# Experts of two mixture-of-experts blocks in quads: 32 tokens each, a one-hot gather for each quad, and the next quad's gather behind the down projection

## The chip, the cores and the metric

The kernel runs on one core of a Trainium2 chip. Its engines are TensorE (PE, with its weight loads shown as PEld), VectorE (DVE), ScalarE (ACT), GpSimd (POOL) and SyncE (SP), which issues the transfers here. The metric is the device time of one execution in microseconds (us); lower is better.

## The reference

Two transformer stacks one after the other, two layers each, on 256 tokens of width 1024, all in float32. Every layer has a mixer (attention; or retention, RWKV and a short convolution) and then a mixture of 32 experts. What is computed there, for the first stack:

```python
group_p = softmax(xt @ w_group); group_w, group_id = top_k(group_p, 1)
in_group = take_along_axis(expert_logits, group_id)
top_logits, local_id = top_k(in_group, 2)
gates = group_w * softmax(top_logits)
# for each token t and each of its two experts e:
y[t] += gate * ((silu(x[t] @ w_gate[e]) * (x[t] @ w_up[e])) @ w_down[e])
```

In the first stack there are 8 groups of 4 experts, 256 wide inside; in the second 4 groups of 8, 512 wide. So 512 assignments fall on 32 experts, and an expert can get any number of them from 0 to 256. All experts' weights are read in every layer: 100.7 MB in a layer of the first stack, 201.3 MB in one of the second.

## The kernel before

**Weights** come through `ring`, six slots of 2048 KB (a chunk, 4096 floats in each of 128 partitions). SP issues a chunk when `w_used` says that the chunk six before it has been used; PE waits on the slot's `w_loaded`. An expert of the first stack has one chunk of gate and up weights and half a chunk of down weights; one of the second stack has a chunk each for gate, up and down. Six expert chunks are loaded before the expert stage begins.

**`route`** (L1445) finds the two experts of each token, gives each assignment a slot from 1 to 512, sorted by expert, and gathers all 512 rows at once with PE: `xtok` (tokens by features) times `once` (a one-hot of tokens by slots, made by DVE), 16 matmuls of 512 columns (L1501), copied by ACT to `Xs`. DVE builds `by_slot` (gates by slots) and the tables `offs` and `left`.

**`experts`** (L1583) works on pairs of experts in a window of up to 64 tokens each (`WIN`). DVE copies the pair's two windows out of `Xs` to `Xw` (`windows`, L1712). PE multiplies `Xw` by the weights: each expert has 64 columns of the array and 64 rows of the PSUM bank (L1657). One pair of the first stack is 16 such matmuls (gate and up together, 512 wide), one of the second is 16 for gate and 16 for up. Then PE adds the *previous* pair's result into banks 0 to 3 (`combine`, L1639: `Yw` times `gwT`, the gates by tokens), with the turn of `hid` (L1667) and of `gw` (L1672) between, and does the down projection (L1684), second half of the width first. ACT does the silu (L1704), DVE the product (L1727), and both copy results out (L1708, L1740). A float32 matmul stands in the trace as two records, so 16 matmuls are 32 records.

The loop runs `iters` times (8 turns of two pairs in the first stack, 16 turns of one pair in the second), and again for as many rounds as the largest expert needs windows of 64. The order of work on an engine is the order of the code; engines meet only at semaphores. In a pair the two chunks of a matmul group are released together at its end, and the chunks of the next groups are already in the ring.

**The ada products** (L756), which the change does not touch, are named since the prediction reads them: they use 32 columns of the array each, four in turn, 512 wide, one chunk for 8 matmuls.

## Time and profile before

| | us |
|---|---|
| median of 3 runs | 3320.39 |
| lowest, highest | 3319.87, 3323.3 |
| span of the profiled execution | 3318.3 |
| PE busy | 2797.8 (84%) |
| DVE busy | 855.7 (26%) |
| ACT busy | 472.3 (14%) |
| gate and up matmuls (L1657), 3072 records | 703.6 |
| down matmuls (L1684), 1536 records | 343.7 |
| sums into banks 0 to 3 (L1639), 1088 records | 263.5 |
| HBM read | 777.00 MB, 234 GB/s over the span |

The profile is of one execution, by the hardware profiler. Busy time is a union: matmuls that run side by side count once. In a timeline row stand the start, the busy time, the engine, the line, the operation with its output and inputs, and the count of records merged in the row; in brackets the engine's idle time before it and what ended it. The granted clock of TensorE is given as a share of 2.4 GHz; it has two levels, 1.2 and 2.4 GHz, so 0.90 over a stretch means that a fifth of it ran at the lower one.

### The profile page before, as it was taken

The page shows a single profiled execution, that of the slowest core. Times are in us where ns is not written, and L with a number is a line of the kernel's source. Part 1 is how long each engine was busy: PE and PEld are TensorE (multiplying, and loading weights), DVE is VectorE, ACT ScalarE, POOL GpSimd, SP SyncE. Part 2 cuts the span into 40 slices and gives each one's busy share as a digit, 9 for nine tenths or more (in the row PEclk, how much of TensorE's full clock was granted, in tenths as well). Part 3 has the DMA queues.
Part 4 walks back from the last instruction along what each step waited for, and adds up shares of the span by engine and source line. Part 5 has one row for each costly group of instructions (what it writes and reads, how often), then busy time and mean ns, then how long its engine had stood idle before and what let it go on. Part 6 is the DMA issues. An engine that isn't in the chain of part 4 may idle for free. (4 is left out here: it accounts for less than half of the span.)

```text
span 3318.3 us, 34187 instructions
## 1 busy us (share of the span) xinstructions
PE 2797.8 (84%) x13108; PEld 1699.9 (51%) x13108; DVE 855.7 (26%) x1849; ACT 472.3 (14%) x879; POOL 0.2 (0%) x4
## 2 busy tenths in 40 slices
PE   6869997868996994869898889869858797988886
PEld 4544445544443852858743333347547686333333
DVE  1442221343122126351121111111364312110111
ACT  1311110321111002200111011010121001101111
POOL 0000000000000000000000000000000000000000
PEclk9889998888998997969989999989978798999998
DMA  6015995114994553003349999864700032899994
GB/s 266 32 54 215 428 419 217 51 46 166 427 428 189 236 192 163 1 1 129 150 191 429 428 429 428 374 276 166 289 1 1 26 152 105 368 429 429 428 429 206
DMA packets 55690, 779.39 MB, mean 235 GB/s; under 512 B 6825, under 2 KB 7081, under 8 KB 7849
## 3 DMA queue, kind: packets, MB, share of 16 engines
q1 hardware_dynamic: 55592, 778.07, 56.4%
q8 instruction: 64, 1.05, 0.1%
q14 instruction: 34, 0.27, 0.0%
HBM read 777.00 MB, written 1.05 MB: 234 GB/s over the span
## 5 line engine op out<-in xcount | busy, mean ns | idle before, releaser
L1657 PE MATMUL bank<-ring,arena 128*64 128x512 f32 x3072 | 703.6, 612 | 84.6 <-issue 70.1
L1657 PEld LDWEIGHTS bank<-ring,arena 128*64 128x64 f32 x3072 | 240.8, 141 | 538.7 <-issue 538.4
L1684 PE MATMUL bank<-ring,arena 128*64 128x512 f32 x1536 | 343.7, 596 | 0.0
L1639 PE MATMUL bank<-arena 128*128 128x256 f32 x1088 | 263.5, 386 | 3.6 <-DVE arena L1740 3.6
L1639 PEld LDWEIGHTS bank<-arena 128*128 128x128 f32 x1088 | 196.1, 190 | 80.2 <-issue 58.9
L1727 DVE TENSOR_TENSOR arena<-bank,arena 128x256 f32<-128x256 f32 (+1 forms) x64 | 35.7, 558 | 776.6 <-ACT arena L1704 776.6
L825 PE MATMUL bank<-xnT,ring 128*128 128x256 f32 x960 | 211.4, 383 | 9.3 <-PEq L271 9.3
L1684 PEld LDWEIGHTS bank<-ring,arena 128*64 128x64 f32 x1536 | 104.6, 137 | 193.5 <-issue 193.5
L825 PEld LDWEIGHTS bank<-xnT,ring 128*128 128x128 f32 x960 | 184.6, 193 | 35.9 <-issue 10.3
L1357 PE MATMUL bank<-xnT,ring 128*128 128x256 f32 x768 | 177.1, 384 | 23.8 <-PEq L962 23.8
L1357 PEld LDWEIGHTS bank<-xnT,ring 128*128 128x128 f32 x768 | 148.1, 193 | 46.1 <-issue 25.4
L1704 ACT ACTIVATE arena<-bank 128x256 f32<-128x256 f32 (+1 forms) x64 | 31.4, 491 | 843.7 <-PE bank L1657 843.7
L295 PE MATMUL bank<-arena,cst 128*128 128x256 f32 x160 | 51.2, 490 | 85.9 <-ACT arena L280 85.9
L1740 DVE COPY arena<-bank 128x512 f32<-128x512 f32 x64 | 44.3, 692 | 305.1 <-PE bank L1684 305.1
L1364 PE MATMUL bank<-arena,ring 128*128 128x256 f32 x384 | 90.7, 379 | 0.0
L295 PEld LDWEIGHTS bank<-arena,cst 128*128 128x128 f32 x160 | 39.6, 254 | 98.9 <-ACT arena L280 91.3
L674 PE MATMUL bank<-arena,ring 128*128 128x256 f32 x256 | 59.7, 398 | 33.5 <-DVE arena L688 33.5
L819 PE MATMUL bank<-ring,xnT 128*128 128x512 f32 x192 | 82.7, 592 | 0.0
L1501 PE MATMUL bank<-arena 128*128 128x512 f32 x128 | 63.7, 661 | 19.7 <-DVE arena L1554 19.7
L831 DVE COPY arena<-bank 128x512 f32<-128x512 f32 x20 | 13.8, 692 | 249.2 <-PE bank L825 176.8
L1364 PEld LDWEIGHTS bank<-arena,ring 128*128 128x128 f32 x384 | 73.0, 190 | 9.9
L1708 ACT COPY arena<-bank 128x512 f32<-128x512 f32 x64 | 37.5, 586 | 269.0 <-PE bank L1684 269.0
(335 smaller groups left out, 2822.9 us busy)
## 6 DMA issues: line engine op xcount, KB each, us to landing
ring<-in_w_exp SPq DMA_DIRECT2D x288, 2048.0 KB, 15.5
ring<-in_w_ada SPq DMA_DIRECT2D x24, 2048.0 KB, 7.9
ring<-in_w_in SPq DMA_DIRECT2D x20, 2048.0 KB, 11.3
ring<-in_w_merge SPq DMA_DIRECT2D x18, 2048.0 KB, 17.1
ring<-in_w_o SPq DMA_DIRECT2D x8, 2048.0 KB, 16.4
ring<-in_w_conv SPq DMA_DIRECT2D x6, 2048.0 KB, 27.5
ring<-in_w_rest SPq DMA_DIRECT2D x2, 1696.0 KB, 21.1
small<-in_small SPq DMA_DIRECT2D x2, 1440.0 KB, 22.9
```

The source lines that it names most:

```text
L295: last = nc.tensor.matmul(sums[:, 0:T], K("ones"), sq[:, k, :], start=k == 0, stop=k == KT - 1)
L674: last = nc.tensor.matmul(bank[b][:, T * (j % 2):T * (j % 2) + T], w[:, k, P * j:P * j + P], mixT[:, k, :], start=k == 0, stop=k == KT - 1)
L819: last = nc.tensor.matmul(o[:, 0:MW], xnT[:, k, P * (not first):P * (not first) + P], w[:, k, :], start=k == 0, stop=k == KT - 1)
L825: last = nc.tensor.matmul(o[:, T * j:T * j + T], w[:, k, col:col + P], xnT[:, k, :], start=k == 0, stop=k == KT - 1)
L1357: last = nc.tensor.matmul(bank[m % 8][:, 0:T], w[:, k, P * (d % 4):P * (d % 4) + P], xnT[:, k, :], start=k == 0, stop=k == KT - 1)
L1364: last = nc.tensor.matmul(bank[m % 8][:, T:2 * T], w[:, k, P * d:P * d + P], ys[i][:, k, :], start=k == 0, stop=k == MT - 1)
L1501: last = nc.tensor.matmul(bank[gather_banks[d]][:, :], xtok[:, t, P * d:P * d + P], once[:, t, :], start=t == 0, stop=t == TT - 1)
L1639: nc.tensor.matmul(bank[d // 2][:, T * (d % 2):T * (d % 2) + T], Yw[:, P * d:P * d + P], gwT, start=False, stop=False, skip_group_check=True)
L1657: last = nc.tensor.matmul(o[rows(e), 0:MW], Xw[:, k, WIN * e:WIN * e + WIN], ring[:, slot(n), MW * k:MW * k + MW], start=k == 0, stop=k == ...
L1684: last = nc.tensor.matmul(o[rows(e), :], hidT[:, j, WIN * e:WIN * e + WIN], ring[:, slot(n), at:at + MW], start=j == 0, stop=j == ft - 1)
L1708: nc.scalar.copy(Yw[:, MW:D], y1_bank[:, :]).then_inc(y1_taken, 1)
L1740: nc.vector.tensor_copy(Yw[:, 0:MW], y0_bank[:, :]).then_inc(y0_taken, 1)
```

## The change

`route` and `experts` become one function, `moe` (L1447 of the new file). Experts run four at a time ("quad"), each in a window of 32 tokens: 32 columns of the array and 32 rows of the bank. What one pass over a quad does is an *item*. A quad whose largest expert has more than 32 tokens gets a second item (and so on), with its weights kept in the ring; the number of items and each item's quad are worked out by DVE from the counts, and read from `offs` and `meta` by the other engines.

There is no gather of all tokens. Each item has a one-hot of its own (`onehot`, tokens by 128 slots, made by DVE from a table of ranks), and PE gathers with 16 matmuls of 128 columns (L1535), into banks 6 and 7; the gather of the next item stands behind the down projection. ACT and DVE copy the halves to `Xw`. Gate, up and down of all four experts run with the experts inside the loop over k, so in the second stack an item is a group of 32 matmuls on four chunks for gate, the same for up, the same for down. The weights in memory are laid out in quads; the ring keeps its six slots. The sum of the previous item now stands in one piece ahead of the turn of `hid`. The zeroing of banks 0 to 3 moves ahead of the ranks, the last matmul that only closed the sum is gone, and the last additions to `hT` start bank by bank.

```diff
-        WIN = 64
+        WIN = 32
+        QUAD = 4
+        NQ = NE // QUAD
         ROUNDS = T // WIN
-        SLOTS = 2 * T
...
+        ITEMS = NQ + 2 * T // WIN
+        xtok = ar(0, TT, D)
+        Xw = ar(2048, KT, P)
...
+                    sp.wait_ge(tables_ready, 1)
+                    for q in range(NQ):
+                        if q:
+                            earlier = sp.value_load(offs[0:1, LAST_AT + q - 1:LAST_AT + q], min_val=0, max_val=ITEMS * per_turn)
+                        if per_turn > RING:
+                            same = sp.value_load(offs[0:1, LAST_AT + q:LAST_AT + q + 1], min_val=0, max_val=ITEMS * per_turn)
+                        for n in range(RING if q == 0 else 0, per_turn):
+                            if n < RING:
+                                sp.wait_ge(w_used, earlier + (n0 + n + per_turn - RING + 1))
+                            else:
+                                sp.wait_ge(w_used, same + (n0 + n - RING + 1))
+                            sp.dma_start(ring[:, slot(n), :], feed(q, n)).then_inc(w_loaded[slot(n)], 16)
...
+                    def gather():
+                        for d in range(KT):
+                            for t in range(TT):
+                                last = nc.tensor.matmul(gather_banks[d // 4][:, P * (d % 4):P * (d % 4) + P], xtok[:, t, P * d:P * d + P], onehot[:, t, :],
+                                                        start=t == 0, stop=t == TT - 1)
+                            if d == 3:
+                                last.then_inc(low_gathered, 1)
+                        last.then_inc(high_gathered, 1)
...
+                        pe.wait_ge(low_taken, it + 1)
+                        pe.wait_ge(high_taken, it + 1)
+                        pe.wait_ge(y1_taken, it + 1)
+                        for o, first in ((gate_bank, 0),) if shared else ((gate_bank, 0), (up_bank, QUAD)):
+                            if first:
+                                pe.wait_ge(y0_taken, it + 1)
+                            for e in range(QUAD):
+                                here(first + e)
+                            for k in range(KT):
+                                for e in range(QUAD):
+                                    last = nc.tensor.matmul(o[rows(e), :], Xw[:, k, rows(e)], ring[:, slot(first + e), MW * k:MW * k + MW],
+                                                            start=k == 0, stop=k == KT - 1)
+                                    if k == KT - 1:
+                                        last.then_inc(w_used, 1)
+                        pe.wait_ge(y0_taken, it + 1)
+                        pe.wait_ge(gwT_ready, it + 1)
+                        combine()
+                        pe.wait_ge(hid_made, it + 1)
+                        for j in range(ft):
+                            last = nc.tensor.transpose(gate_bank[:, P * j:P * j + P], hid[:, P * j:P * j + P], K("ident"))
+                        last.then_inc(hid_turned, 1)
+                        pe.wait_ge(gw_ready, it + 1)
...
+                        pe.wait_ge(hidT_ready, it + 1)
+                        for n in range(n_gu, per_turn):
+                            here(n)
+                        for half, o in ((1, y1_bank), (0, y0_bank)):
+                            if half == 0:
+                                pe.wait_ge(gwT_ready, it + 2)
+                            for j in range(ft):
+                                for e in range(QUAD):
+                                    n, at = (n_gu + e // 2, ft * D * (e % 2)) if shared else (n_gu + e, 0)
+                                    at += D * j + MW * half
+                                    last = nc.tensor.matmul(o[rows(e), :], hidT[:, j, rows(e)], ring[:, slot(n), at:at + MW], start=j == 0, stop=j == ft - 1)
+                                    if half == 0 and j == ft - 1 and (e % 2 == 1 or not shared):
+                                        last.then_inc(w_used, 1)
+                            if half == 1:
+                                last.then_inc(y1_done, 1)
+                        if more:
+                            pe.wait_ge(onehot_ready, it + 2)
+                            gather()
...
+                    then(nc.vector.tensor_reduce(most, count.rearrange("p (q e) -> p q e", e=QUAD), AX, ALU.max))
+                    then(nc.vector.tensor_scalar(most, most, 1.0 / WIN, None, ALU.mult))
+                    then(nc.vector.tensor_tensor(more, most.unsqueeze(2).broadcast_to([P, NQ, ROUNDS - 1]), iota[:, 0:ROUNDS - 1].unsqueeze(1).broadcast_to([P, NQ, ROUNDS - 1]), ALU.is_gt))
+                    then(nc.vector.tensor_reduce(rounds, more, AX, ALU.add))
+                    then(nc.vector.tensor_scalar(rounds, rounds, 1.0, None, ALU.add))
...
-                                for k in range(KT):
-                                    for e, n in enumerate((wa, wb)):
-                                        last = nc.tensor.matmul(o[rows(e), 0:MW], Xw[:, k, WIN * e:WIN * e + WIN], ring[:, slot(n), MW * k:MW * k + MW],
-                                                                start=k == 0, stop=k == KT - 1)
-                                        if k == KT - 1:
-                                            last.then_inc(w_used, 1)
...
+                        if more:
+                            dve.wait_ge(low_gathered, it + 1)
+                            dve.wait_ge(high_gathered, it + 1)
+                            dve.wait_ge(gw_ready, it + 1)
+                            off = dve.value_load(offs[0:1, bass.ds(RANK_AT + it + 1, 1)], min_val=0, max_val=NE * TT * ROUNDS - QUAD * TT)
+                            slots_of(rank_tab[:, bass.ds(off, QUAD * TT)])
```

Of PE's instructions in the second stack's expert loop, before (L1657 gate, then up; L1639 the sum; L1667 and L1672 turns; L1684 down, its two halves):

```order
L1657 MATMUL bank<-ring,arena 64x512 x16
L1645 REGISTER_ALU
L1657 MATMUL bank<-ring,arena 64x512 x16
L1639 MATMUL bank<-arena 128x256 x4
L1667 MATMUL bank<-cst,arena 128x128 x4
L1639 MATMUL bank<-arena 128x256 x4
L1672 MATMUL bank<-cst,arena 128x128 x2
L1684 MATMUL bank<-ring,arena 64x512 x8
L1680 REGISTER_ALU
L1684 MATMUL bank<-ring,arena 64x512 x8
```

and in the changed kernel (L1567 gate and up, L1543 the sum, L1576 and L1580 turns, L1592 down, L1535 the next gather):

```order
L1567 MATMUL bank<-ring,arena 32x512 x64
L1543 MATMUL bank<-arena 128x256 x8
L1576 MATMUL bank<-cst,arena 128x128 x4
L1580 MATMUL bank<-cst,arena 128x128 x2
L1555 REGISTER_ALU
L1592 MATMUL bank<-ring,arena 32x512 x16
L1587 REGISTER_ALU
L1592 MATMUL bank<-ring,arena 32x512 x16
L1535 MATMUL bank<-arena 128x128 x16
```

The count of matmuls per expert is the same (8 for gate, 8 for up, 8 for down); a loop turn now holds four experts for two, the sum comes once a turn in one piece, and the gather has moved into the loop.

The same engine between the router's logits and the first expert, before:

```order
L1484 MATMUL bank<-cst,xnT 128x128 x16
L1490 MATMUL bank<-arena,cst 128x32
L1491 MATMUL bank<-arena,cst 128x32
L1492 MATMUL bank<-arena,cst 128x32
L1494 MATMUL bank<-arena,cst 128x32 x2
L1501 MATMUL bank<-arena 128x512 x16
L1468 UNCONDITIONAL_BRANCH
L1634 UNCONDITIONAL_BRANCH
L1642 MATMUL bank<-cst 128x512 x4
L1607 TENSOR_LOAD meta
```

and in the changed kernel:

```order
L1516 MATMUL bank<-cst,xnT 128x128 x16
L1519 MATMUL bank<-cst 128x512 x4
L1525 MATMUL bank<-arena,cst 128x32
L1526 MATMUL bank<-arena,cst 128x32
L1527 MATMUL bank<-arena,cst 128x32
L1529 MATMUL bank<-arena,cst 128x32 x2
L1535 MATMUL bank<-arena 128x128 x16
L1480 TENSOR_LOAD meta
```

The zero matmuls (L1642, now L1519) stand ahead of the ranks, the gather is a quarter as wide, and no block ends between it and the experts.

## Rows read from the trace of the kernel before

**Rows 1.** The page: its first line, and the rate in 40 slices.
```profile
span 3318.3 us, 34187 instructions
GB/s 266 32 54 215 428 419 217 51 46 166 427 428 189 236 192 163 1 1 129 150 191 429 428 429 428 374 276 166 289 1 1 26 152 105 368 429 429 428 429 206
```

**Rows 2.** Windows: length, busy time of five engines, PEclk, DMA share, GB/s.
```profile
400.00:420.00 20.00, 20.00 (x94) 9.35 (x91) 3.73 (x9) 1.73 (x4) 0.00 (x0) 1.00 1.01 429
...
500.00:520.00 20.00, 17.79 (x80) 9.39 (x76) 4.30 (x11) 1.34 (x3) 0.00 (x0) 1.00 0.00 0
...
1800.00:1900.00 100.00, 91.29 (x412) 37.50 (x410) 10.51 (x22) 11.03 (x14) 0.00 (x0) 0.97 1.01 428
```

**Rows 3.** Timeline: start and end of an expert stage of each stack, SP's first issue.
```profile
280.37 7.09 PE L1657 MATMUL bank<-ring,arena 128*64 128x512 f32 x32
...
287.78 7.92 SPq L1624 DMA_DIRECT2D ring<-in_w_exp  x3
...
518.71 2.73 DVE L1745 TENSOR_TENSOR hT<-hT,bank 128x256 f32<-128x256 f32 x8 [4.73 <-PE bank L1694]
...
1696.88 13.96 PE L1657 MATMUL bank<-ring,arena 128*64 128x512 f32 x64
...
2163.52 3.23 DVE L1747 SCALAR_TENSOR_TENSOR hT<-bank,mod,hT 128x256 f32<-128x256 f32 x8 [4.73 <-PE bank L1694]
```

**Rows 4.** Two chunk issues of L187 by themselves: start, and time to landing.
```profile
L187 SPq DMA_DIRECT2D ring<-in_w_ada x1: 333/333/333, 2297.8 to 2297.8; - x1
DMA to landing us min/median/max: 7.8/7.8/7.8
...
L187 SPq DMA_DIRECT2D ring<-in_w_ada x1: 333/333/333, 2304.7 to 2304.7; - x1
DMA to landing us min/median/max: 7.7/7.7/7.7
```

**Rows 5.** Timeline of PE in the ada products, 32-column matmuls, lower and full clock.
```profile
1069.93 3.35 PE L756 MATMUL bank<-ring,arena 128*32 128x512 f32 x16 [3.03 <-DMA ring<-in_w_ada]
...
1074.82 1.93 PE L756 MATMUL bank<-ring,arena 128*32 128x512 f32 x16 [0.56 <-DMA ring<-in_w_ada]
```

**Rows 6.** Timeline of PE in the second stack, two phases after waits.
```profile
2960.98 7.09 PE L1657 MATMUL bank<-ring,arena 128*64 128x512 f32 x32 [1.22 <-DMA ring<-in_w_exp]
2970.73 8.74 PE L1657 MATMUL bank<-ring,arena 128*64 128x512 f32 x32 [2.66 <-issue]
```

**Rows 7.** Windows that start with dense matmuls after a wait.
```profile
33.00:53.00 20.00, 19.96 (x80) 17.16 (x81) 0.69 (x1) 0.59 (x1) 0.00 (x0) 0.86 1.01 428
...
259.80:279.80 20.00, 19.01 (x39) 8.21 (x40) 8.89 (x36) 5.55 (x10) 0.00 (x0) 0.90 0.01 2
```

**Rows 8.** Windows soon after the expert transfers start, first stack's second layer.
```profile
825.00:830.00 5.00, 5.00 (x26) 3.75 (x26) 2.27 (x6) 0.76 (x2) 0.00 (x0) 1.00 0.99 383
830.00:835.00 5.00, 5.00 (x26) 1.59 (x23) 0.73 (x2) 0.59 (x1) 0.00 (x0) 1.00 1.00 413
```

**Rows 9.** Timeline at the end of the first layer's experts.
```profile
505.50 1.99 PE L1639 MATMUL bank<-arena 128*128 128x256 f32 x8
...
509.59 3.65 PE L1684 MATMUL bank<-ring,arena 128*64 128x512 f32 x16
...
514.13 3.69 PE L1639 MATMUL bank<-arena 128*128 128x256 f32 x16 [0.89 <-DVE arena L1740]
```

**Rows 10.** Timeline of the first layer's routing.
```profile
250.39 3.53 PE L1484 MATMUL bank<-cst,xnT 128*128 128x128 f32 x16
...
255.07 0.19 DVE L1542 COPY arena<-bank 128x32 f32<-128x32 f32 x1 [1.99 <-PE bank L1494]
...
257.27 0.48 DVE L1553 TENSOR_SCALAR arena<-arena 128x512 f32<-128x512 f32 x1
...
259.88 15.97 PE L1501 MATMUL bank<-arena 128*128 128x512 f32 x32 [4.92 <-DVE arena L1554]
...
276.76 3.67 PE L1642 MATMUL bank<-cst 128*128 128x512 f32 x8 [0.92 <-PEq L1468]
```

More of the change, by code:

```diff
@@ L1458, in route, with slot, items, used @@
             gs, ge, pen = (ar(at + 100 + 16 * i, TT, ng) for i in range(3))
[L1459 to L1467 removed]
+            gtop, gsum, coef = (ar(at + 160 + 2 * i, TT, 1) for i in range(3))
+            z, zs, ez, sel = (ar(at + 200 + 64 * i, TT, NE) for i in range(4))
+            v8 = ar(at + 520, TT, 8)
+            d21 = ar(at + 540, TT, 1)
+            count = ar(at + 560, NE)
+            most, rounds, cum = (ar(at + 600 + 8 * i, NQ) for i in range(3))
+            more = ar(at + 640, NQ, ROUNDS - 1)
+            past = ar(at + 720, ITEMS + 1, NQ)
+            quad_of, before_it = (ar(at + 930 + 32 * i, ITEMS + 1) for i in range(2))
+            gate_bank, up_bank = bank[4], bank[4 if shared else 5]
+            y1_bank, y0_bank = bank[4], bank[5]
+            gather_banks = (bank[6], bank[7])
+            iota = K("iota")
+            def slot(n):
+                return (n0 + n) % RING
+            def items(eng):
+                return eng.value_load(meta[0:1, 0:1], min_val=NQ, max_val=ITEMS)
+            def used(eng, it, n):
+                eng.wait_ge(w_used, it * per_turn + (n0 + n + 1))
+            def rows(e):
+                return slice(WIN * e, WIN * e + WIN)
             with nc.Block() as block:
@@ L1495, in _ @@
                     last.then_inc(rank_ready, 1)
-                    pe.wait_ge(tok_taken, 4)
-                    pe.wait_ge(once_ready, TT)
-                    for d in range(KT):
-                        for t in range(TT):
-                            last = nc.tensor.matmul(bank[gather_banks[d]][:, :], xtok[:, t, P * d:P * d + P], once[:, t, :], start=t == 0, stop=t == TT - 1)
-                        last.then_inc(gathered, 1)
+                    def gather():
[6 more added lines that the diff above has]
+                        last.then_inc(high_gathered, 1)
@@ new lines, in combine @@
+                    def combine(ready=None):
+                        for d in range(KT):
+                            last = nc.tensor.matmul(bank[d // 2][:, T * (d % 2):T * (d % 2) + T], Yw[:, P * d:P * d + P], gwT, start=False, stop=ready is not None, skip_group_check=True)
+                            if ready is not None and d % 2:
+                                last.then_inc(ready, 1)
+                    pe.wait_ge(onehot_ready, 1)
+                    gather()
+                    pe.wait_ge(tables_ready, 1)
@@ L1503, in _, with take_token @@
+                    n_items = items(pe)
+                    with pe.Fori(0, n_items - 1) as it:
+                        item(it, True)
+                    item(n_items - 1, False)
+                    pe.wait_ge(y1_taken, n_items + 1)
+                    pe.wait_ge(y0_taken, n_items + 1)
+                    combine(sum_ready)
                 @block.scalar
                 def _(act):
+                    def take_token(i):
+                        act.wait_ge(tok_turned, i + 1)
+                        nc.scalar.copy(xtok[:, i // 2, MW * (i % 2):MW * (i % 2) + MW], bank[(6, 7, 4, 5)[i]][:, :]).then_inc(tok_taken, 1)
@@ L1742, in _ @@
+                    n_items = items(dve)
+                    with dve.Fori(0, n_items - 1) as it:
+                        item(it, True)
+                    item(n_items - 1, False)
                     for d in range(KT):
+                        dve.wait_ge(sum_ready, d // 2 + 1)
                         y = bank[d // 2][:, T * (d % 2):T * (d % 2) + T]
@@ L1816, in build @@
                 norm("n2b", gains[:, 1, :], mod[:, 24:32], 11000)
[L1817 to L1818 removed]
+                moe("e2", lambda q, n: dram["w_exp2"][l, 12 * q + n], MOE2, F2, wr2, NG2, row[0:1, 0:R2_N], mod[:, 40:48])
                 zero_semaphores()
```

331 lines of the change are left out of this document (123 added, 208 removed).

## The prediction

> **What bounds the kernel now.** I read the page first, then the windows over the expert stages, then the timeline at their edges. The page gives a span of 3318.3 us and, in slices, 428 or 429 GB/s wherever experts run [rows 1]. The windows say the same more finely: 429 GB/s in the first stack's experts and 428 over 100 us of the second's, with PE nearly always at work beside it [rows 2]. A chunk of 2048 KB is 2.097 MB, so at 428.5 GB/s one chunk takes 4.9 us, and nothing makes that shorter. In the first stack two pairs of experts (one turn, six chunks, 29.4 us of transfer) also cost PE about 29 us: PE goes on after the last transfer, with the queue at 0 GB/s from 500 us [rows 2]. In the second stack a pair is six chunks and PE waits for them. So both stacks sit at or close to the transfer bound. Fewer matmul slots can buy little; what matters is whether the change keeps the queue full.
>
> From the first expert matmul to the last addition a stage takes 518.71 + 2.73 - 280.37 = 241.1 us in the first stack and 2163.52 + 3.23 - 1696.88 = 469.9 us in the second [rows 3], twice each.
>
> **Edit 1: matmuls on a quarter of the array.** Two 64-column matmuls share a slot now; 32 records take 7.09 us [rows 3]. The trace has 32-column, 512-wide matmuls too, in the ada products at L756: 16 records in 1.93 us with a full clock [rows 5], so four run side by side. A gate or up phase of four experts has 64 records: 1.93 + 12 x 0.43 (a slot, 1.93 less a tail of 0.2, by 4) = 7.1 us. Halving PE's expert time is real, but it is worth only what PE now costs beyond the transfers.
> The Trainium skill, "TensorE: Matmul & The Clock Gate", Part 3 (measured speedup of packed matmuls), gives 3.07x for four tiles, not 4x. By that the phase would be an estimated 9.2 us; rows 5 speak for the full factor.
>
> **Edit 2: chunks are released four at a time.** This is the term that decides. The new loop goes over k outside and over four experts inside, so all four chunks of a phase are released at its very end, and the ring has only six slots. While such a phase runs, just two more chunks can be on their way: 2 x 4.9 = 9.8 us of cover. What must fit under that cover:
> - PE's phase and SP's reaction: first matmul 280.37, next issue 287.78, so 7.4 us warm [rows 3], plus 0.1 to wake up after a landing: 7.5.
> - The landing of the chunk then issued. On an idle queue it comes 7.6 to 7.8 us after the issue. At 2304.7 a chunk was issued when the one before (issued 2297.8, landed 7.8 later, 2305.6) had 0.9 us to go; it still took 7.7 us, so its landing came 6.8 us after its neighbour's instead of 4.9 [rows 4]. Hence an issue must lie 7.7 - 4.9 = 2.8 us before the previous landing, or the queue runs dry.
> Warm, 7.5 + 2.8 = 10.3 against 9.8: dry by half a microsecond in each phase. Before, two chunks were released at a time and four others stayed in the ring, which is why 429 GB/s stood. SP issues strictly in order, so behind its wait for the first of the four stand the other three and the rest of the quad. Between quads it now also reads one or two registers; they stand where it would wait for a release anyway, or behind two chunks of the same release, so I take them at nothing (0 to 0.5 us a quad if not, inside b's bounds).
>
> **Edit 3: the phases are now islands.** Between two phases of the second stack PE waits for two new chunks, 7.7 + 4.9 = 12.6 us after its release. It fills at most 5 us (the sum into banks 0 to 3, or the gather). A wait of 2.66 us was enough to turn a 7.09 us phase into 8.74 [rows 6], a loss of 1.65 us. After longer waits the granted clock averages 0.90 and 0.86 over the first 20 us of dense work [rows 7]; with levels of 1.2 and 2.4 GHz that is 2.0 and 2.8 us lost. I take c = 2.1, nearest to the gather's 2.0 (also 512-wide), and keep 1.65 to 2.8. Every phase pays c, and since it is exposed under Edit 2 it pays in full.
> Added to this, a refilled queue is not at once at full rate: 383 and 413 GB/s in windows after a restart, all with DMA engines busy [rows 8], that is 0.5 and 0.2 us per 5 us. I take b = 0.5 us a restart, bounds 0 and 1.2 (the sum over one whole start-up, with a margin).
>
> From the landing that starts a phase to the landing of the first new chunk it is then 7.45 + 7.65 = 15.1 us, plus c + b = 2.6: 17.7 us.
> - Second stack, a quad has three such phases (gate, up, down), each needing two new chunks: 17.7 + 4.9 = 22.6 us, against 19.6 of transfer. There are 8 x 3 = 24 phases, 23 steps: 519.8 us. After the last phase starts: 0.1 + 7.1 + 2.1, the copy 0.9, the sum 3.7 [rows 9], and 1.1 for the last two additions, which now run bank by bank: 15.0. Stage 534.8 against 469.9: +64.9, two layers +129.8.
> - First stack, a quad has one four-chunk phase and then needs four new ones: 17.7 + 3 x 4.9 = 32.4 us against 29.4. Its down phase falls inside this. Seven steps are 226.8; the end is 9.3 + 4.1 (combine and turns, 505.50 to 509.59) + 3.65 + 0.9 + 3.7 [rows 9] + 0.9 = 22.5. Stage 249.3 against 241.1: +8.2 a layer.
> - The token limit. Windows of 32 instead of 64 make a second item of a quad where an expert has more than 32 tokens. Going through the routing of the reference's own inputs, the largest experts of the four layers have 29, 38, 31 and 23 tokens; so the four stages have 8, 9, 8 and 8 items. The ninth is a second turn of the first quad in a layer of the first stack, all its chunks held meanwhile: 7.1 + 4.1 + 3.65 + 3.5 (gather) + 0.8 (copy) = +19.2.
>
> **Edit 4: routing.** Out go the gather of all tokens (15.97 us of PE), the tables by slot, the block's end and the windows' copies; PE's first expert matmul comes 280.37 - 275.85 = 4.5 us after that gather [rows 10]. In comes a gather of one quad: 32 records of 128 columns, 3.5 us warm or 6.8 cold. The zero matmuls (3.67 us) move before the ranks, where they are in the open, up to 6.8 us cold. DVE's new tables come to some 25 small operations after that gather; such ones take 0.24 us now (nine from 255.07 to 257.27, [rows 10]; where one need not wait for another, half): 5 to 6 us exposed, since PE waits for them. From the end of the turns (253.9): 3.4 to 6.8 zeros, 1.1 ranks, 1 one-hot, 3.5 to 6.8 gather, 0.7 copy, 5.5 tables, 1.5 register loads make 270.6 to 277.3, against 280.4. I take 8 saved, bounds 3 and 10: -32 for four layers. This hides under nothing, and neither did what it replaces. The gathers for later quads (3.5 us each) lie in PE's waits and cost nothing; without those waits they would cost 29 x 3.5 = 102 us.
>
> **Sum.** 129.8 + 8.2 + 8.2 + 19.2 - 32 = +133.4, on 3318.3: 3451.7 us of span. The median of the runs lies 2.1 us above this span, so 3454 us.
>
> "DMA: Bandwidth & Descriptors" of the Trainium skill, Anatomy of one DMA, gives a fixed cost of some 2.0 us for its path, where the row leaves 2.8. With 2.0 each restart would be 0.8 us shorter, and the estimate 3406. The row decides.
>
> **Rivals.**
> A. *The queue never runs dry*, faster. If PE stayed warm and the refill had no cost (c = b = 0), the second stack would be 23 x 20.0 + 12.9 = 473 us, the first 7 x 29.8 + 20.4 = 229, plus 19.2 once, and routing still -32: about 3289 us. It needs c + b under 0.4 us (133 us by some 60 restarts is 2.2 of the 2.6). Rows 6 and 7 speak against it: no resumption after a wait was free. Chance 0.10.
> B. *Four tiles do not run four abreast* when their moving rows come from four ring slots, or their loads get in the way. The phase grows by 2.1 us (the 3.07x of the page above would do this), exposed 64 times: 3454 + 134 = 3588. Rows 5 are against it. Chance 0.05.
> C. *More items than I count*: an expert with 31 tokens in the second stack gets two more by rounding on the chip. One item there is 3 x 7.1 + 4 + 3.5 + 1, some 30 us: 3484, inside the range. Chance 0.03. That the change does not do what it says is ruled out by the order of PE's rows shown above: 64 matmuls of 32 columns in a row where there were 32 of 64.
>
> **How the numbers follow.** The forecast has 0.80, a time within 0.2% (c + b near 0.4) 0.02. With c + b at 1.65 and at 4.0 instead of 2.6, 60 restarts and four tails give 3395 and 3545; some sixty restarts average the clock's scatter, so I cut the upper end to 3520, and put the lower one at 3390, for routing at its better bound. This leaves out A, B and the rest, under 0.2. A measurement of this kernel tells some 0.2% (7 us) from no change. Faster: A, 0.10. Same: 0.02. Slower: forecast, B and C, 0.88.
>
> **What would show it.** In the profile after: in the second stack 22 to 23 us from phase to phase, GB/s near 375 instead of 428 in its windows; PE idle 8 to 13 us before each phase on a chunk; a granted clock that falls before every phase, and phases of 8.6 to 10 us; PE's matmul time for experts about halved; nine items in the second layer; a routing stage of 29 us. I am wrong if the second stack still moves 428 GB/s, if phases after a wait take 7.1 us, or if a chunk issued within 1 us of the last landing arrives sooner than 7 us.

## The result: 3.0% slower, as forecast, and a little less so

The changed kernel takes 3422.23 us (median of 4 runs, 3418.57 to 3425.36) against 3320.42 for the kernel before on the same chip: a ratio of 1.0303, 95% interval 1.0288 to 1.0318. The forecast was 3454, range 3390 to 3520, so sign, mechanism and range held, and the size was 32 us too large. One run of hold_release below took 5886.34 us, where its other three took 3257.05 to 3261.01, and is left out of its figures. Late and one_item were run twice, the other changed kernels four or five times.

The page of the changed kernel: its first line, the granted clock and the rate in 40 slices, and the two groups of expert matmuls with the idle time before them.

```profile
span 3423.6 us, 33363 instructions
...
PEclk9978888888888997879877777789987898777777
...
GB/s 264 25 49 295 398 337 258 2 49 241 391 398 258 156 279 16 1 28 157 99 379 379 375 376 376 307 292 166 252 1 1 76 170 142 377 388 380 377 377 203
...
L1567 PE MATMUL bank<-ring,arena 128*32 128x512 f32 x3136 | 451.4, 740 | 524.5 <-DMA ring<-in_w_exp 493.2
...
L1592 PE MATMUL bank<-ring,arena 128*32 128x512 f32 x1568 | 210.5, 693 | 141.8 <-DMA ring<-in_w_exp 137.7
```

Where [rows 1] had 428 and 429 GB/s in the second stack's experts, 375 to 388 stand now. PE's gate, up and down matmuls fell from 703.6 + 343.7 us to 451.4 + 210.5, and PE waits 493.2 + 137.7 us for chunks. That is 37% less, not the half that the prediction gave as a sign of itself: warm it would be half, but nearly every gate and up phase, and every down phase of the second stack, runs partly at the lower clock. More than a third of PE's expert time is gone and the kernel is slower: a sign that this work was not what bounded it.

The first and the last window of [rows 2] again; in the second shown, PE is busy 51.74 us of 100 where it was 91.29.

```profile
400.00:420.00 20.00, 17.01 (x128) 9.39 (x120) 3.08 (x6) 3.21 (x5) 0.00 (x0) 0.96 0.87 358
1800.00:1900.00 100.00, 51.74 (x361) 23.30 (x363) 6.01 (x11) 6.67 (x9) 0.00 (x0) 0.76 0.92 381
```

One quad of the second stack in the timeline of the changed kernel: gate, up, the sum (L1543), down (L1592), the gather of the next quad (L1535), and the next gate.

```profile
1832.93 9.81 PE L1567 MATMUL bank<-ring,arena 128*32 128x512 f32 x64 [9.12 <-DMA ring<-in_w_exp]
...
1842.88 46.36 SPq L1502 DMA_DIRECT2D ring<-in_w_exp  x12
1855.54 8.75 PE L1567 MATMUL bank<-ring,arena 128*32 128x512 f32 x64 [12.80 <-DMA ring<-in_w_exp]
1864.22 3.72 PE L1543 MATMUL bank<-arena 128*128 128x256 f32 x16
...
1877.14 9.89 PE L1592 MATMUL bank<-ring,arena 128*32 128x512 f32 x64 [8.54 <-DMA ring<-in_w_exp]
...
1886.96 3.84 PE L1535 MATMUL bank<-arena 128*128 128x128 f32 x32
...
1899.72 1.08 PE L1567 MATMUL bank<-ring,arena 128*32 128x512 f32 x4 [8.92 <-DMA ring<-in_w_exp]
```

Three steps, each from the start of one phase to the start of the next, from 1832.93 to 1899.72 are 66.8 us, 22.3 each (forecast 22.6; the transfer of four chunks is 19.6). No phase is short: 9.81, 8.75, 9.89 us where a warm one would be 7.1, and each follows a wait of 8.5 to 12.8 us. The phase that starts at 1832.93 ends at 1842.74; SP issues at 1842.88, and not before.

By stage, from the first router matmul, the first expert matmul and the end of the last addition in the timelines (us):

| stage | before | after | difference | forecast |
|---|---|---|---|---|
| routing, four layers | 149.4 | 111.6 | -37.8 | -32 |
| experts, first stack, layer 1 | 241.1 | 247.2 | +6.2 | +8.2 |
| experts, first stack, layer 2 (nine items) | 241.1 | 266.3 | +25.3 | +27.4 |
| experts, second stack, layer 1 | 469.9 | 528.8 | +58.9 | +64.9 |
| experts, second stack, layer 2 | 469.9 | 525.4 | +55.6 | +64.9 |
| everything else | | | -2.7 | 0 |
| span | 3318.3 | 3423.6 | +105.3 | +133.4 |

### The profile page after: what moved, and what is told of

Read it like the earlier page. It is cut to its first block and busy times, and to the rows that moved or that the text cites. A ratio compares the mean times of both kernels' runs of the same rounds, so it can differ in the third digit from the quotient of the medians.

```text
span 3423.6 us, 33363 instructions
## 1 busy us (share of the span) xinstructions
PE 2349.3 (69%) x13472; PEld 1518.2 (44%) x13473; DVE 732.4 (21%) x1535; ACT 399.4 (12%) x768; POOL 0.2 (0%) x4
## 5 line engine op out<-in xcount | busy, mean ns | idle before, releaser
L1567 PE MATMUL bank<-ring,arena 128*32 128x512 f32 x3136 | 451.4, 740 | 524.5 <-DMA ring<-in_w_exp 493.2
L1567 PEld LDWEIGHTS bank<-ring,arena 128*32 128x32 f32 x3136 | 123.9, 132 | 828.2 <-issue 828.2
L1592 PE MATMUL bank<-ring,arena 128*32 128x512 f32 x1568 | 210.5, 693 | 141.8 <-DMA ring<-in_w_exp 137.7
L1738 DVE TENSOR_TENSOR arena<-bank,arena 128x256 f32<-128x256 f32 (+1 forms) x33 | 18.3, 554 | 908.4 <-PE bank L1567 613.1
L1592 PEld LDWEIGHTS bank<-ring,arena 128*32 128x32 f32 x1568 | 56.5, 125 | 273.8 <-issue 265.6
L1543 PE MATMUL bank<-arena 128*128 128x256 f32 x592 | 137.5, 385 | 3.8 <-DVE arena L1746 3.8
L1535 PEld LDWEIGHTS bank<-arena 128*128 128x128 f32 x1056 | 120.4, 192 | 28.2 <-issue 24.3
L1543 PEld LDWEIGHTS bank<-arena 128*128 128x128 f32 x592 | 109.4, 190 | 48.4 <-issue 35.0
L1535 PE MATMUL bank<-arena 128*128 128x128 f32 x1056 | 126.7, 278 | 3.4 <-DVE arena L1654 3.4
L1746 DVE COPY arena<-bank 128x512 f32<-128x512 f32 x33 | 22.8, 691 | 311.6 <-PE bank L1592 311.6
L1635 ACT ACTIVATE arena<-bank 128x256 f32<-128x256 f32 (+1 forms) x33 | 16.1, 487 | 594.9 <-PE bank L1567 594.9
L1365 PEld LDWEIGHTS bank<-arena,ring 128*128 128x128 f32 x384 | 73.0, 190 | 9.9
L675 PEld LDWEIGHTS bank<-arena,ring 128*128 128x128 f32 x256 | 51.4, 202 | 43.2 <-DVE arena L689 35.4
## 6 DMA issues: line engine op xcount, KB each, us to landing
ring<-in_w_rest SPq DMA_DIRECT2D x2, 1696.0 KB, 19.6
```

The source lines that it names most:

```text
L675: last = nc.tensor.matmul(bank[b][:, T * (j % 2):T * (j % 2) + T], w[:, k, P * j:P * j + P], mixT[:, k, :], start=k == 0, stop=k == KT - 1)
L1365: last = nc.tensor.matmul(bank[m % 8][:, T:2 * T], w[:, k, P * d:P * d + P], ys[i][:, k, :], start=k == 0, stop=k == MT - 1)
L1535: last = nc.tensor.matmul(gather_banks[d // 4][:, P * (d % 4):P * (d % 4) + P], xtok[:, t, P * d:P * d + P], onehot[:, t, :], start=t == 0 ...
L1543: last = nc.tensor.matmul(bank[d // 2][:, T * (d % 2):T * (d % 2) + T], Yw[:, P * d:P * d + P], gwT, start=False, stop=ready is not None, ...
L1567: last = nc.tensor.matmul(o[rows(e), :], Xw[:, k, rows(e)], ring[:, slot(first + e), MW * k:MW * k + MW], start=k == 0, stop=k == KT - 1)
L1592: last = nc.tensor.matmul(o[rows(e), :], hidT[:, j, rows(e)], ring[:, slot(n), at:at + MW], start=j == 0, stop=j == ft - 1)
```

## The experiments

The theory: an item's phase (the gate, up or down matmuls of one quad) waits for four chunks and frees four at its end; with six slots only two are then on their way, so the queue runs dry, and whatever PE spends in the phase, the lost clock included, lies on the path. Rivals: the transfers, the narrow matmuls or the layout are slow by themselves; release or wait alone does the harm; the clock is not what makes the phases long. Each run is compared with the kernel before on the same chip (3317 to 3320 us).

| run | us | ratio to before (95%) | first stack, stages | second stack, stages |
|---|---|---|---|---|
| changed kernel | 3422 | 1.0303 (1.0288 to 1.0318) | 247.2, 266.3 | 528.8, 525.4 |
| slices | 3233 | 0.9744 (0.9727 to 0.9760) | 220.9, 241.3 | 456.1, 456.2 |
| hold_wait | 3253 | 0.9805 (0.9790 to 0.9820) | 226.6, 245.5 | 464.0, 464.2 |
| hold_release | 3257 | 0.9820 (0.9802 to 0.9838) | 226.2, 246.1 | 462.9, 462.9 |
| hold_both | 3417 | 1.0306 (1.0284 to 1.0328) | 247.3, 265.0 | 525.4, 525.3 |
| pairs | 3279 | 0.9877 (0.9859 to 0.9894) | 231.8, 257.3 | 466.6, 467.0 |
| late | 3545 | 1.0679 (1.0658 to 1.0701) | 262.1, 286.6 | 566.0, 566.1 |
| filled | 3348 | 1.0090 (1.0073 to 1.0107) | 233.8, 264.1 | 499.2, 497.9 |
| one_item | 3404 | 1.0262 (1.0228 to 1.0296) | 247.1, 247.4 | 525.3, 525.3 |
| early_tables | 3211 | 0.9675 (0.9656 to 0.9694) | 219.8, 238.3 | 454.5, 454.5 |

### slices: wait and release chunk by chunk

```diff
-                            for e in range(QUAD):
-                                here(first + e)
                             for k in range(KT):
+                                if k % 2 == 0:
+                                    here(first + k // 2)
                                 for e in range(QUAD):
-                                    ... ring[:, slot(first + e), MW * k:MW * k + MW] ...
-                                    if k == KT - 1:
-                                        last.then_inc(w_used, 1)
+                                    at = MW * QUAD * (k % 2) + MW * e
+                                    ... ring[:, slot(first + k // 2), at:at + MW] ...
+                                if k % 2 == 1:
+                                    last.then_inc(w_used, 1)
```

(`...` stands for code left out.) The down phase likewise: j outside, one chunk for each j, the two halves of the width inside.

> The changed kernel, with the weights laid out another way: a chunk of a phase now holds one quarter of the depth (two k, or one j) for all four experts, where it held all of it for one expert. So PE waits for, uses and releases the chunks one by one, with the same matmuls on the same data. Theory (four chunks released at once with six slots let the queue run dry): the queue stays full. Second stack: first landing 9.7 us into the stage, 89 more at 4.88 us, 7.5 us of work behind the last: 452 us a stage, down from 529 and 525. First stack: 9.7 + 41 x 4.88 + 6.6 = 216 us, and 236 with the ninth item, from 247 and 266. Together about -211 us: 3211 us. Rival 1 (the narrow matmuls or the gather in the loop are the cost): as the changed kernel, 3422. Rival 2 (the clock falls in the waits and PE itself becomes the limit): a cold phase is 14.2 us, still under the 19.5 of its four chunks, so this rival has to show PE waits that end on something other than a transfer, and a stage over 500 us.

Measured 3233.01 us, 22 more than expected; each of the four stages took 4 to 5 us longer than that. The first landing comes 11.5 to 12.1 us into a stage (the layer with nine items aside), not 9.7, and the landings are 4.91 us apart on average, not 4.88. The timeline in the down phase of an item of the second stack, and the window over 100 us:

```profile
1846.96 1.92 PE L1591 MATMUL bank<-ring,arena 128*32 128x512 f32 x16 [0.53 <-ACT arena L1636]
...
1849.99 1.92 PE L1591 MATMUL bank<-ring,arena 128*32 128x512 f32 x16 [1.11 <-DMA ring<-in_w_exp]
1854.88 3.45 PE L1591 MATMUL bank<-ring,arena 128*32 128x512 f32 x16 [2.97 <-DMA ring<-in_w_exp]
1859.76 1.92 PE L1591 MATMUL bank<-ring,arena 128*32 128x512 f32 x16 [1.42 <-DMA ring<-in_w_exp]
```

```profile
1800.00:1900.00 100.00, 61.67 (x414) 20.97 (x418) 5.15 (x9) 6.69 (x9) 0.00 (x0) 0.86 1.01 429
```

PE now works in quarters of a phase at the pace of the chunks, 4.9 us apart, and 429 GB/s is back. Some quarters still run at the lower clock (3.45 us instead of 1.92), and it costs nothing, because the next chunk is not there yet. Same matmuls, same gather, same bytes: 189 us less. So neither the narrow matmuls, nor the gather, nor the transfers by themselves are to blame.

### hold_wait, hold_release, hold_both: which half of it does the harm

In `slices`, hold_wait puts the wait for all four chunks back ahead of the phase; hold_release puts the release of all four back to its end; hold_both does both. The release as in hold_release and hold_both, for gate and up (cut):

```diff
                             for k in range(KT):
                                 ...
-                                if k % 2 == 1:
-                                    last.then_inc(w_used, 1)
+                                if k == KT - 1:
+                                    last.then_inc(w_used, QUAD)
```

> The kernel with sliced chunks (run slices), but PE waits for all four chunks of a phase before its first matmul, as in the changed kernel; it still releases them one by one. Theory: the first release comes 2 us after the phase starts, with 9.8 us of transfer on its way, so the queue stays full. Only the end of a stage is longer, since a whole phase (7.1 us warm, 9.3 after a wait) stands behind the last landing instead of 1.9: 462 us a stage in the second stack, 223 and 243 in the first, together 3249 us. Rival (the wait for four at a time costs by itself, since PE sits cold between phases): near the changed kernel's 3422.

> The kernel with sliced chunks (run slices), but the chunks of a phase are released all four at its end, as in the changed kernel; PE still waits for them one by one. Theory: it is release and wait together that empty the queue. With the wait by slice PE has only the last quarter of the phase (1.9 us) to do when the fourth chunk lands, so the release still comes 7.9 us before the two chunks on their way are in, and the queue stays full. Only the first issue of a stage is 5.2 us later: 461 us a stage in the second stack, 226 and 247 in the first, together 3254 us. Rival (releasing four at once costs by itself, whatever the wait): near the changed kernel's 3422.

> The kernel with sliced chunks, but with both the wait for all four and the release of all four at the end. It differs from the changed kernel only in how the weights lie in the chunks and in the order of the down phase (width inside, depth outside). Theory: the layout is nothing by itself, so stages of 529, 525, 247 and 266 us and 3422 us come back, within 10. Rival (the sliced layout is what helped, for example since four matmuls abreast now read one slot): it stays near 3233.

Measured 3253, 3257 and 3417 us, within 6 us of each expectation. Timeline of hold_wait: SP's issue comes 3.8 us after the phase starts, inside it, and the phase itself is as slow as in the changed kernel.

```profile
1844.81 9.04 PE L1568 MATMUL bank<-ring,arena 128*32 128x512 f32 x64 [10.98 <-DMA ring<-in_w_exp]
1848.63 39.48 SPq L1502 DMA_DIRECT2D ring<-in_w_exp  x9
```

Timeline of hold_release, a gate phase: SP's issue comes at its end (1840.52), but only 2.1 us after the fourth chunk was in (1838.40).

```profile
1838.40 1.92 PE L1568 MATMUL bank<-ring,arena 128*32 128x512 f32 x16 [1.37 <-DMA ring<-in_w_exp]
...
1840.52 43.16 SPq L1502 DMA_DIRECT2D ring<-in_w_exp  x12
```

The same window in hold_wait, hold_release and hold_both, in this order: full rate, full rate, not.

```profile
1800.00:1900.00 100.00, 58.77 (x406) 23.76 (x406) 5.83 (x11) 6.87 (x10) 0.00 (x0) 0.80 1.01 429
```

```profile
1800.00:1900.00 100.00, 66.07 (x444) 25.57 (x436) 6.70 (x12) 6.87 (x10) 0.00 (x0) 0.88 1.01 429
```

```profile
1800.00:1900.00 100.00, 58.16 (x406) 23.45 (x398) 5.16 (x9) 6.69 (x9) 0.00 (x0) 0.77 0.91 373
```

So the wait for four alone and the release of four alone cost 4 to 8 us a stage each, with the rate in the middle of the stage at its full value. The release costs at the start: SP's first issue of a second-stack stage comes 9.2 us after the first expert matmul in hold_release (1668.00 against 1658.76), 3.9 us in slices. Only together do they put a whole phase between the last landing and the next issue. With both, the whole of the changed kernel's slowness is back in a kernel with the other layout, so the layout is nothing by itself. Hold_wait shows one thing more: its phases are cold (8.4 to 10.0 us in the second stack, granted clock 0.80 over the window) and its rate is 429, so the lower clock costs only where the phase is exposed.

### pairs: two chunks at a time, at twice the matmul time

```diff
-                            for e in range(QUAD):
-                                here(first + e)
-                            for k in range(KT):
-                                for e in range(QUAD):
+                            for pair in ((0, 1), (2, 3)):
+                                for e in pair:
+                                    here(first + e)
+                                for k in range(KT):
+                                    for e in pair:
                                         ...
```

The down phase likewise.

> The changed kernel with its chunks as they are, but each phase done for experts 0 and 1 first and then for 2 and 3: two chunks awaited and released at a time, two matmuls abreast instead of four, so a phase takes twice as long on PE (14.2 us). Theory of the release: second stack at the transfer's pace in spite of twice the matmul time, 462 us a stage (from 529 and 525); first stack PE-bound, 14.2 + 5.2 + 7.3 + 4.6 = 31.3 us an item, about 250 and 281 us (from 247 and 266). Sum -112: about 3310 us. Rival (time follows PE's work, not the release): three phases of 7.1 us more in each item of the second stack, 8 x 21 = +170 us a stage, over 3700 us.

Measured 3279 us. The second stack is as expected (466.6 and 467.0 for 462). The first is 18 and 24 us shorter than expected:

```profile
341.22 0.38 PE L1577 MATMUL bank<-cst,arena 128*128 128x128 f32 x2
...
342.07 5.38 PE L1594 MATMUL bank<-ring,arena 128*32 128x512 f32 x32 [0.24 <-ACT arena L1639]
```

The down phase takes 5.38 us, not 7.3. Of its 32 records, those from 343.81 to 345.14 start in fours instead of twos, so by the order of the code the last matmuls of experts 0 and 1 run beside the first of experts 2 and 3, in other columns of the array. Where no wait for a chunk stands in an item it comes to 26.8 us (782.01 to 808.77 in the timeline), less than the 29.4 of its transfers, so the first stack is not PE-bound as I had it. Slower matmuls, 144 us faster than the changed kernel: that rules out PE's work as the cause.

### late: 1.7 us more in each phase

```diff
                             for k in range(KT):
+                                if k == KT - 1:
+                                    filler(2)
                                 for e in range(QUAD):
```

`filler(n)` is n matmuls of zeros added into banks 0 to 3; the same ahead of the last j of the down phase in the second stack.

> The changed kernel with two matmuls of zeros (1.7 us) inside each gate, up and down phase of the second stack and each gate-and-up phase of the first, ahead of the last k or j, so that the release of the four chunks comes 1.7 us later. Theory (PE's phase is exposed one for one since the queue is dry by then): 65 phases x 1.7 = +111 us, about 3533 us. Rival (the transfers are slower by themselves, PE has slack): +15 us at most, for the tails.

Measured 3545 us, +123 for +111 expected; the four stages give +15, +20, +37 and +41, 113 us for 111; the other 10 us lie outside the expert stages and stay unexplained. One for one within the stages, then; the rival's +15 is out.

### filled: is it the clock?

```diff
                             pe.wait_ge(onehot_ready, it + 2)
                             gather()
+                            filler(13 if shared else 8)
```

`filler` as in late, and 14 behind a gate phase, 8 ahead of the down phase in the second stack.

> The changed kernel with matmuls of zeros added into banks 0 to 3 (which leaves the sum as it is) wherever PE waits for chunks: 14 behind a gate phase, 8 ahead of the down phase, 8 behind the gather in the second stack, 13 behind the gather in the first, 0.857 us each, so PE is never idle for long but not late either. Theory (the clock falls in the wait and 2.2 us of every phase are lost to it, exposed): phases of 7.1 us instead of 9.3, steps of 20.1 us instead of 22.2 in the second stack and 29.7 instead of 31.8 in the first, -51 and -15 us a stage, +11 once where the ninth item had no wait: about 3300 us. Rival (a phase is long for another reason, such as the load of 32-column tiles or the ring's slots): phases stay at 9.3 us and the time at 3422 or above.

Measured 3348 us: 74 us less than the changed kernel, where 122 were expected. Its timeline, two phases of the second stack with the fillers (L1553) between:

```profile
2065.06 12.28 PE L1553 MATMUL bank<-cst 128*128 128x512 f32 x28
...
2065.28 23.26 SPq L1502 DMA_DIRECT2D ring<-in_w_exp  x8
2078.15 7.07 PE L1571 MATMUL bank<-ring,arena 128*32 128x512 f32 x64 [0.81 <-DMA ring<-in_w_exp]
```

Of the 32 gate and up phases of the second stack 21 now take under 7.5 us (none did before), and their mean is 7.7 for 9.3. The granted clock over 1800 to 1900 us is 0.98, where the changed kernel has 0.76. So the clock is what made the phases long. This gains 1.6 us a phase, but a step of the second stack became only 1.2 us shorter. (The 11 us of fillers in the ninth item, which had no wait to hide them, were part of the expectation, and did come.) Some phases are still cold, and the rest went into the next term. The issues of the changed kernel around a release, one with the queue nearly empty and the one before it (1844.6 + 20.6 = 1865.2 is its landing):

```profile
L1502 SPq DMA_DIRECT2D ring<-in_w_exp x1: 332/332/332, 1864.4 to 1864.4; - x1
...
DMA to landing us min/median/max: 7.7/7.7/7.7
```

```profile
L1502 SPq DMA_DIRECT2D ring<-in_w_exp x1: 332/332/332, 1844.6 to 1844.6; - x1
...
DMA to landing us min/median/max: 20.6/20.6/20.6
```

The same in filled; the chunk before lands at 2067.4 + 20.4 = 2087.8, that is 2.5 us after the issue:

```profile
L1502 SPq DMA_DIRECT2D ring<-in_w_exp x1: 333/333/333, 2085.3 to 2085.3; - x1
...
DMA to landing us min/median/max: 8.3/8.3/8.3
```

```profile
L1502 SPq DMA_DIRECT2D ring<-in_w_exp x1: 333/333/333, 2067.4 to 2067.4; - x1
...
DMA to landing us min/median/max: 20.4/20.4/20.4
```

Over all expert chunks of a run, by how long before the previous landing a chunk was issued (the lead), from the issue and landing of each (means; a negative lead is an issue after that landing):

| lead, us | run | chunks | issue to landing | landing to landing |
|---|---|---|---|---|
| -2 to -1 | late | 50 | 7.78 | 9.29 |
| -1 to 0 | changed kernel | 24 | 7.73 | 8.10 |
| 0 to 1 | changed kernel | 28 | 7.76 | 7.00 |
| 2 to 3 | filled | 40 | 8.40 | 5.96 |
| 3 to 4 | filled | 4 | 8.53 | 5.05 |
| 5 to 6 | before | 11 | 10.57 | 4.91 |
| 5 to 6 | hold_wait | 49 | 10.80 | 4.97 |

With a lead of 2 to 3 us the gap would be 7.75 - 2.5 = 5.25 if the chunk came as on an empty queue; it is 5.96. As the release gets earlier, the gain shrinks before the rate is full.

### one_item: what the ninth item costs

```diff
-then(nc.vector.tensor_scalar(most, most, 1.0 / WIN, None, ALU.mult))
+then(nc.vector.tensor_scalar(most, most, 0.0, None, ALU.mult))
```

> The changed kernel with the tokens of every quad measured by 0 instead of 1/32, so that each quad gets one item and tokens beyond an expert's 32nd are left out (six tokens of one expert in the second layer). Theory: eight items everywhere, the second layer's stage falls from 266.3 to 247.2 us like the first's, 19 us in all: 3403 us. Rival (the ninth item hides behind transfers and the second layer's stage is long for another reason): 3422, stage of 266.

Measured 3404 us, the second layer's stage 247.4 for 266.3: 18.9 us. (This kernel leaves out the tokens beyond an expert's 32nd.)

### early_tables: the routing term

DVE's work behind the first one-hot in another order, in `slices` (in parentheses, what the lines left out do):

```diff
+                    (tables of items, tables_ready)
+                    dve.wait_ge(high_gathered, 1)
+                    take_high()
                     (sum of the groups, coef, gate_tab, weigh)
-                    dve.wait_ge(high_gathered, 1)
-                    take_high()
-                    (tables of items, tables_ready)
```

> The kernel with sliced chunks (run slices), with DVE's work behind the first one-hot in another order: the tables of items first, then its half of the gathered tokens, then the gates. In run slices PE's first expert matmul (1646.38) waits for the tables, which DVE begins only after its copy of the gather (1639.26) and ends at 1644.5. Theory of the routing term (about 5 us of tables exposed): they now run beside the gather (3.84 us), and the first expert matmul comes 4.4 us earlier in each of four layers: 3233 - 17 = 3216 us. Rival (the way from the tables to the first matmul, register loads included, is long whatever comes before): routing stages of 27 to 28 us as now, 3233.

Measured 3211 us. Timeline of slices, then of early_tables: PE's gather, DVE's copy of its second half, the end of the tables, the first expert matmul.

```profile
1635.38 3.84 PE L1535 MATMUL bank<-arena 128*128 128x128 f32 x32 [0.85 <-DVE arena L1653]
...
1639.26 0.69 DVE L1661 COPY arena<-bank 128x512 f32<-128x512 f32 x1 [2.38 <-PE bank L1535]
...
1644.47 0.06 DVE L1724 MEMSET spare<- 128x1 f32 x1
...
1646.38 4.29 PE L1568 MATMUL bank<-ring,arena 128*32 128x512 f32 x20 [7.16 <-issue]
```

```profile
1624.84 3.84 PE L1535 MATMUL bank<-arena 128*128 128x128 f32 x32 [0.85 <-DVE arena L1653]
...
1629.55 0.06 DVE L1711 MEMSET spare<- 128x1 f32 x1
...
1629.65 0.69 DVE L1661 COPY arena<-bank 128x512 f32<-128x512 f32 x1
...
1631.46 8.79 PE L1568 MATMUL bank<-ring,arena 128*32 128x512 f32 x80 [2.78 <-issue]
```

From the start of the gather to the first expert matmul it is 6.6 us instead of 11.0. With slices this is the fastest kernel of the study, 3.3% under the one before.

## Why the forecast was right, and where it was off

**What bounds the kernel** was read rightly: the transfers. Pairs and late show it from both sides: 7 us more of matmul in a phase of the second stack with an early release, 144 us faster; 1.7 us more ahead of the release, 123 us slower.

**The matmul's price** was right: 7.07 us for 64 records (filled, and the ninth item's phase after a wait of 1.14 us) against 7.1 worked out from the ada products. By the 3.07x of the Trainium skill, "TensorE: Matmul & The Clock Gate", Part 3, it would have been an estimated 9.2; the trace does not agree with it here. The page measured that figure for four tiles of 32 rows, where these are four tiles of 32 columns. The phases of the changed kernel do average 9.3 us, but for another reason, as filled shows. Rival B fell, though a glance at the mean alone would have seemed to confirm it.

**Release and wait by four** was right, with one correction: the prediction gave the release as the term that decides. Hold_release has the same release and runs at 429 GB/s. It is the release at the end *and* a wait for the last of the four that together make a whole phase fall between a landing and an issue.

**c, the clock's loss in a phase**, forecast 2.1 us, is 2.2 in the second stack (mean 9.27, less 7.07). In the first the mean is 9.10; without the ninth item's warm phase it is 9.23, so 2.2 again.

**b, the refilled queue, is the step that failed.** It was taken as 0.5 us a restart, some 60 times, so 30 us of the forecast. In the changed kernel it is about zero: behind the 52 first landings with a lead of -1 to 1 us the next one follows after 4.88 us on average, and the first comes 7.75 us after its issue, for which the sum had already put 7.65. I had taken [rows 8] for a queue that had just been refilled. In the timeline of before SP's first issue of that stage stands far ahead of them (the chunk lands at 804.2), and the windows right behind that landing are full:

```profile
796.60 37.01 SPq L1624 DMA_DIRECT2D ring<-in_w_exp  x9
```

```profile
800.00:805.00 5.00, 5.00 (x25) 1.76 (x25) 1.45 (x3) 0.59 (x1) 0.00 (x0) 1.00 1.00 429
805.00:810.00 5.00, 5.00 (x26) 1.72 (x24) 0.00 (x0) 0.00 (x0) 0.00 (x0) 1.00 1.03 436
```

So 383 GB/s at 825 has another cause than a restart; which one stays open. By step: 22.3 us instead of 22.6 in the second stack, 31.8 instead of 32.4 in the first, about 22 us over the 60 restarts.

The latency itself was right at the lead where it was needed: [rows 4] gave 7.7, the changed kernel 7.75. "DMA: Bandwidth & Descriptors" of the Trainium skill, Anatomy of one DMA, with its 2.0 us of fixed cost, would give an estimated 6.9; the measurement says 2.85 on top of the 4.9, as the row did. That section is on transfers that GpSimd issues, and these are issued by SP, so the two do not contradict each other; the figure was only not the one to use here. That its estimate of 3406 lies nearer to 3422 than my 3454 is two errors that cancel, that fixed cost and my b.

**Rival A**, the queue that never runs dry, needed c + b under 0.4. Filled took most of c away and gained 74 of the 102 us by which the changed kernel is slower: even with a nearly full clock the kernel stays slower than before, since b then comes back as 0.7 us (5.96 less 5.25). The real way to A is not a faster phase but an earlier issue, as slices shows.

**The token limit**, +19.2: the two layers of the first stack differ by 19.1, and one_item takes 18.9 away.

**Routing**, -32, came out at -37.8, 9.5 a layer instead of 8, inside its bounds of 3 and 10. The rows of the changed kernel in the first layer: zeros, gather, DVE's copy, the end of the tables, the first expert matmul.

```profile
249.43 4.53 PE L1519 MATMUL bank<-cst 128*128 128x512 f32 x8
...
255.85 3.84 PE L1535 MATMUL bank<-arena 128*128 128x128 f32 x32 [0.85 <-DVE arena L1654]
...
259.72 0.69 DVE L1662 COPY arena<-bank 128x512 f32<-128x512 f32 x1 [2.37 <-PE bank L1535]
...
264.95 0.06 DVE L1725 MEMSET spare<- 128x1 f32 x1
...
267.33 1.08 PE L1567 MATMUL bank<-ring,arena 128*32 128x512 f32 x4 [7.65 <-issue]
```

The gather was warm (3.84 of 3.5 to 6.8) and the zeros nearly so (4.53, and 3.60 in the second stack, of 3.4 to 6.8); the tables took 4.6 us from the end of the copy, a little under the 5 to 6 forecast, and 2.3 us more went by to the first expert matmul, for 1.5 of register loads. The values in the middle had allowed for more cold work than there was.

**Errors that met.** By stage the forecast was too high by 15.3 us in the second stack, 4.2 in the first, 5.8 in routing and 2.7 elsewhere: 28 us, all of one sign. Only the 19.5 us of the expert stages have to do with b and c (30 too much for the one, some 6 too little for the other, and a few us spread over the stages). That the whole miss is as large as b's 30 is chance: the routing and the rest happened to err the same way.

## What to carry to other kernels

Under a ring of few slots, look at the stretch between the landing that completes a wait and the next issue, and keep it shorter than the transfers still on their way less the lead that an issue needs ahead of the previous landing (about 3 us here, at 2 MB a chunk): wait late or release early, and one of the two is enough. A ring of more slots, the other way to more cover, was not tried. A kernel that waits for its transfers gains nothing from a faster phase unless the phase lies in that stretch; there each microsecond counts in full, lost clock included, until the queue is nearly full again. To run several operands side by side in the array, lay the data out so that a chunk holds a slice of all of them, not all of one: this alone turned +3.0% into -2.6%.

## What the runs showed of the hardware that was not expected

- A 2 MB chunk issued 2 to 3 us before the previous one lands does not come as if the queue were free: issue to landing grows from 7.75 to 8.40 us. Of the four chunks in filled with a lead of 3 to 4 us, three come 4.7 to 4.9 us after the one before and one 5.64, so the lead that is needed lies near 3 us.
- The lower clock was harmless where something else set the pace: hold_wait has a granted clock of 0.80 over 100 us and moves 429 GB/s there.
- Two groups of 32-column matmuls that use different columns overlap at their seam: 5.38 us for the down phase in pairs, where two abreast throughout would be 7.1.
